# One encoder layer on one core: the first value tiles are computed token tile by token tile, ahead of the queries and keys

## The reference

```python
u = rmsnorm(h, g_pre_mix)
proj = u @ w_in                       # 512 x 3840
qa, ka, va, qb, kb, vb, qc, kc, vc = split(proj)
ya = diff_attention(qa, ka, va, ...)  # branch A: 4 heads, two softmaxes each
yb = sliding_window_sink_attention(qb, kb, vb, ...)   # branch B: 8 heads
yc = chunk_band_attention(qc, kc, vc, ...)            # branch C: 8 heads
mixed = gates[0] * (ya @ w_proj_a) + gates[1] * (yb @ w_proj_b) + gates[2] * (yc @ w_proj_c)
h = h + rmsnorm(mixed @ w_out, g_post_mix)
h = h + rmsnorm(conv_ffn(rmsnorm(h, g_pre_ffn), ...), g_post_ffn)
```

## Time and profile before

| | |
|---|---|
| time, median of 3 runs | 844.48 us (843.78 to 846.26) |
| the profiled execution | 843.84 us, its span 842.0 us |
| TensorE busy | 833.5 us (99%) |
| VectorE busy | 653.8 us (78%) |
| ScalarE busy | 481.5 us (57%) |
| GpSimd busy | 400.1 us (48%) |
| DMA | 111.35 MB, mean 132 GB/s |

### The profile page before, as it was taken

The page is one execution under the profiler, slowest core; times in us unless marked ns, Lnnn a source line. Parts: engine busy times, 40 slices in busy tenths (PEclk is TensorE's granted clock), DMA queues, the critical chain, the costliest instruction groups (busy, mean ns, idle before and its releaser), DMA issues.

```text
span 842.0 us, 13461 instructions
## 1 busy us (share of the span) xinstructions
PE 833.5 (99%) x4721; PEld 729.3 (87%) x4721; DVE 653.8 (78%) x1257; ACT 481.5 (57%) x906; POOL 400.1 (48%) x511
## 2 busy tenths in 40 slices
PE   8999999999999999999999999999999999999997
PEld 7888888888888888999998889899999999988885
DVE  6678877788866767966544389988888888999996
ACT  6566666777666664544444447456565656545662
POOL 5554443334444446987667435756565656010002
PEclk9999999999999999999999999999999999999999
DMA  8542223233233212333335641555553433396584
GB/s 229 158 121 55 64 86 99 75 98 82 83 82 81 62 41 88 113 110 110 107 101 206 198 147 51 172 175 179 162 178 112 131 110 129 132 329 219 172 285 157
DMA packets 139079, 111.35 MB, mean 132 GB/s; under 512 B 7591, under 2 KB 122223, under 8 KB 137732
## 3 DMA queue, kind: packets, MB, share of 16 engines
q1 hardware_dynamic: 137386, 102.05, 39.8%
q0 software_dynamic: 720, 5.24, 1.7%
q10 hardware_dynamic: 906, 3.20, 1.0%
HBM read 97.05 MB, written 13.42 MB: 131 GB/s over the span
## 4 chain that ended last, share of the span: by engine, by line
PE 94%; DVE 2%; POOL 1%; DMA 1%; ACT 1%; issue 1%; DVEq 0%; SPq 0%; ACTq 0%
PE banks L2280 23%; PE banks L2282 23%; PE banks L2281 23%; PE banks L2557 3%; PE banks L2556 3%; PE banks L2555 3%; PE banks L2456 2%; PE banks L2365 2%; PE banks L2364 2%; PE banks L2726 1%; PE banks L2725 1%; PE banks L2724 1%; PE banks L2428 1%; PE banks L2435 1%; PE banks L2419 1%; DVE scratch L1976 1%
## 5 line engine op out<-in xcount | busy, mean ns | idle before, releaser
L856 POOL TENSOR_TENSOR ring_lo<-ring_raw,ring_hi 128x256 fp32r<-128x256 f32 x376 | 307.2, 850 | 262.8 <-ACT ring_hi L1014 262.4
L2280 PE MATMUL banks<-u_hi,ring_hi 128*128 128x512 f32 (+1 forms) x612 | 231.3, 378 | 0.5 <-POOL ring_lo L880 0.5
L2282 PE MATMUL banks<-u_hi,ring_lo 128*128 128x512 f32 (+1 forms) x612 | 226.4, 370 | 0.0
L2281 PE MATMUL banks<-u_lo,ring_hi 128*128 128x512 f32 (+1 forms) x612 | 226.1, 370 | 0.0
L2282 PEld LDWEIGHTS banks<-u_hi,ring_lo 128*128 128x128 f32 x612 | 115.2, 188 | 20.2
L2280 PEld LDWEIGHTS banks<-u_hi,ring_hi 128*128 128x128 f32 x612 | 115.4, 189 | 18.6 <-DVE u_lo L1587 0.8
L2281 PEld LDWEIGHTS banks<-u_lo,ring_hi 128*128 128x128 f32 x612 | 115.6, 189 | 18.0
L1014 ACT CAST ring_hi<-ring_raw 128x1024 fp32r<-128x1024 f32 x95 | 98.9, 1044 | 37.4 <-PE banks L2282 24.1
L2101 DVE SCALAR_TENSOR_TENSOR wide<-banks,cols,wide 128x511 f32<-128x511 f32 x88 | 64.6, 745 | 3.5 <-ACT wide L1374 1.6
L2280 PE MATMUL banks<-pages,ring_hi 128*128 128x512 f32 (+1 forms) x180 | 61.2, 340 | 0.0
L2281 PE MATMUL banks<-pages,ring_hi 128*128 128x512 f32 (+1 forms) x180 | 61.2, 340 | 0.0
(11 more groups left out here) (325 smaller groups left out, 1991.9 us busy)
## 6 DMA issues: line engine op xcount, KB each, us to landing
ring_raw<-in_w_ffn_up_dram SPq DMA_DIRECT2D x88, 256.0 KB, 3.6
ring_raw<-in_w_in_dram SPq DMA_DIRECT2D x60, 256.0 KB, 3.4
ring_raw<-in_w_ffn_down_dram SPq DMA_DIRECT2D x55, 256.0 KB, 3.6
ring_raw<-in_w_gate_dram SPq DMA_DIRECT2D x48, 256.0 KB, 3.2
split_tokens<-pages SPq DMA_DIRECT2D x5, 1024.0 KB, 7.0
pages<-split_tokens POOLq DMA_DIRECT2D x5, 1024.0 KB, 6.5
ring_raw<-in_w_out_dram SPq DMA_DIRECT2D x16, 256.0 KB, 3.1
second_tokens<-wide SPq DMA_DIRECT2D x10, 384.0 KB, 3.9
```

Source lines behind the costliest of these rows:

```text
L856: last = pool.tensor_tensor(wlo[:, r, c], raw[:, r, c], whi[:, r, c].bitcast(F32), ALU.subtract)
L2280: pe.matmul(out, lhs_hi, rhs_hi, start=start, stop=False)
L2281: pe.matmul(out, lhs_hi, rhs_lo, start=False, stop=False)
L2282: return pe.matmul(out, lhs_lo, rhs_hi, start=False, stop=stop)
```

## The change

- Tiles 0 and 1 of the order are `va` and `vb`: the values of units 0 and 1 together, 256 feature columns wide, with rows 0 to 511 of the weights in `va` and rows 512 to 1023 in `vb`.
- Their products (`value_products`) take the tokens as the stationary operand, a token tile of 128 at a time, and 256 weight columns as the moving one. The result stands by tokens, so `v_feat`, `turn_v` and `v_parts` fall away for units 0 and 1; `first_values` evacuates from the bank to the value pages.
- Token tile 0 is turned alone, in two halves, then tiles 1, 2 and 3, each between products of the tiles before.
- SyncE loads x tile 0, then `va`, x tile 1, `vb`, x tiles 2 and 3, then the next two weight tiles. ScalarE rounds tile 0 before it squares token tile 1. The square of token tile 2 is VectorE's.
- Query and key of unit 0 follow at full width (512 tokens), and then `qk(0)`. Four tiles are now computed ahead of the slots, and two more (`SPLIT_AHEAD`) are split ahead of them. The slots get other cuts.
- Idle transposes: 11, 4 and 1 where there were 14, 2 (four times) and 6. Some small loads share a semaphore.

```diff
-SLOT_CUTS = {"A": (0, 5, 11, 17, 24), "C": (0, 5, 10, 16, 24), "B": (0, 6, 11, 17, 24)}
-WARM_UP = (14, 2, 6)
+GEMM_ORDER = ("va0 vb0 q0 k0 q1 k1 v2 q2 k2 v3 q3 k3 v4 q4 k4 v5 q5 k5 v6 q6 k6 v7 q7 k7 v8 k8 q8 "
+              "gate0 q9 gate1 gate2 q10 gate3 gate4 q11 gate5 gate6 gate7")
+SLOT_CUTS = ((0, 5, 11, 17, 23),) + 3 * ((0, 5, 11, 17, 24),) + 4 * ((0, 5, 10, 17, 24),) + (
+    (0, 6, 11, 17, 23), (0, 5, 11, 16, 22), (0, 5, 11, 16, 22), (0, 3, 7, 10, 14))
+SPLIT_AHEAD = RING + 2
+WARM_UP = (11, 4, 1)
...
+        def first_values(g, part, h):
+            page = pages[:, v_page(h, part), :]
+            return tiled(page)[:, g::2, :], psum[:, proj_bank(g), :].rearrange("p (t h n) -> p t h n", t=2, h=2)[:, :, h, :]
...
             load_x(0)
-            load_x(1)
-            load_x(2)
...
+            def by_k_wide(t, r, src):
+                dst = raw[:, r, :].rearrange("p (k n) -> p k n", n=2 * P)
+                load(t, r, (dst[:, 0:2, :], dst[:, 2:4, :]), (src[:, 0:2, :], src[:, 2:4, :]))
...
                 if t == 1:
+                    load_x(1)
+                if t == 2:
+                    load_x(2)
                     load_x(3)
...
             rstd(0, 0)
-            rstd(0, 1)
-            rstd(0, 2)
-            pool.wait_ge(first_half_hi, 1)
+            pool.wait_ge(w_hi_done, 1)
             w_lo_quarter(0, 0)
             w_lo_quarter(0, 1)
-            pool.wait_ge(w_hi_done, 1)
+            rstd(0, 1)
             w_lo_quarter(0, 2)
-            w_lo_quarter(0, 3)
+            w_lo_quarter(0, 3).then_inc(w_lo_done, 1)
+            pool.wait_ge(w_hi_done, 2)
+            w_lo_quarter(1, 0)
+            rstd(0, 2)
...
             square(0, 0, x_tok[:, 0, :])
+            w_hi_at(0)
             act.wait_ge(x_loaded[1], 16)
             square(0, 1, x_tok[:, 1, :])
...
+            act.wait_ge(first_turned, 1)
+            act.copy(u_hi[:, 0:4, 0:P], turned_tokens(0, 0)[:, 0:4, :]).then_inc(u_first_hi, 1)
+            act.wait_ge(xs_turned, 1)
+            act.copy(u_hi[:, 4:8, 0:P], turned_tokens(0, 0)[:, 4:8, :]).then_inc(u_hi_done, 1)
+            w_hi_at(1)
+            u_high(1, 0)
             act.wait_ge(x_loaded[3], 16)
+            act.wait_ge(squares, 3)
             square(0, 3, x_tok[:, 3, :])
-            w_hi_at(1)
+            w_hi_at(2)
             u_high(2, 0)
             u_high(3, 0)
-            w_hi_at(2)
             w_hi_at(3)
...
+            proj_out(0)
             act.wait_ge(lam_dots, 2)
             act.activation(lam_exp[:], lam_dot[:], ACT.Exp).then_inc(lam_exps, 1)
-            proj_out(0)
             proj_out(1)
+            w_hi_at(RING)
             act.wait_ge(dist_done, 2)
...
+            for t in range(RING + 1, SPLIT_AHEAD):
+                w_hi_at(t)
             proj_out(2)
+            proj_out(3)
...
+            xs(0, 1, x_tok[:, 1, :], spread_gain())
+            dve.wait_ge(x_loaded[2], 16)
+            dve.tensor_tensor_reduce(tmp, x_tok[:, 2, :], x_tok[:, 2, :], 1.0, 0.0, ALU.mult, ALU.add,
+                                     norm_ss[:, 0, 2:3]).then_inc(squares, 1)
+            u_low(1, 0)
             for t in (2, 3):
                 xs(0, t, x_tok[:, t, :], spread_gain())
...
+                if kind in ("va", "vb"):
+                    dve.wait_ge(proj_act, g + 1)
+                    for h in range(2):
+                        lo, half = first_values(g, 1, h)
+                        last = dve.tensor_tensor(lo, half, first_values(g, 0, h)[0].bitcast(F32), sub)
+                    last.then_inc(v_lo, 1)
+                    return
...
             tables()
-            for g in range(3):
+            for g in range(RING):
                 proj_low(g)
...
                     pe.wait_ge(proj_act, g - 1)
+                    if g <= RING:
+                        pe.wait_ge(v_lo, 2)
...
+            def value_products(t, u_part, w_part, ks):
+                dst = psum[:, proj_bank(t % 2), 2 * P * (t // 2):2 * P * (t // 2 + 1)]
+                for k in ks:
+                    mm = pe.matmul(dst, u_part[:, k, t * P:(t + 1) * P],
+                                   w_part[:, k // 4, 2 * P * (k % 4):2 * P * (k % 4 + 1)],
+                                   start=u_part is u_hi and w_part is whi and k == 0,
+                                   stop=w_part is wlo and k == KT - 1)
+                return mm
...
+            pe.wait_ge(u_first_hi, 1)
+            pe.wait_ge(w_hi_done, 1)
+            value_products(0, u_hi, whi, first)
+            pe.wait_ge(u_first_lo, 1)
+            value_products(0, u_lo, whi, first)
+            pe.wait_ge(u_hi_done, 1)
+            pe.wait_ge(w_hi_done, 2)
+            value_products(0, u_hi, whi, second)
+            pe.wait_ge(u_lo_done, 1)
+            value_products(0, u_lo, whi, second)
+            pe.wait_ge(w_lo_done, 1)
+            value_products(0, u_hi, wlo, first)
+            turn_tokens(1, 0, x_tok[:, 1, :])
+            pe.wait_ge(u_hi_done, 2)
+            value_products(1, u_hi, whi, both)
+            pe.wait_ge(u_lo_done, 2)
+            value_products(1, u_lo, whi, both)
+            value_products(1, u_hi, wlo, first)
+            turn_tokens(2, 0, x_tok[:, 2, :])
+            pe.wait_ge(w_lo_done, 2)
+            value_products(0, u_hi, wlo, second)
+            value_products(1, u_hi, wlo, second)
+            pe.wait_ge(u_hi_done, 3)
+            value_products(2, u_hi, whi, both)
+            turn_tokens(3, 0, x_tok[:, 3, :])
+            pe.wait_ge(u_lo_done, 3)
+            value_products(2, u_lo, whi, both)
+            value_products(2, u_hi, wlo, both).then_inc(tile_used, 1)
+            turn_tables()
+            pe.wait_ge(u_hi_done, 4)
+            value_products(3, u_hi, whi, both)
+            pe.wait_ge(u_lo_done, 4)
+            value_products(3, u_lo, whi, both)
+            value_products(3, u_hi, wlo, both).then_inc(tile_used, 1)
             gemm_steps(STEPS[-1][2 * KT:])
...
-                if qt == 0 and u <= 8:
+                if qt == 0 and 2 <= u <= 8:
                     turn_v(u)
```

More of the change, by code:

```diff
@@ L464, in build_encoder @@
         x_loaded = [sem(f"x_loaded{t}") for t in range(TT)]
-        small_loaded = [sem(f"small_loaded{i}") for i in range(9)]
+        small_loaded = [sem(f"small_loaded{i}") for i in range(7)]
         raw_loaded = [sem(f"raw_loaded{r}") for r in range(RING)]
@@ L697, in _ @@
             for u in range(4, UNITS - 1):
-                bias_before[min(t for t in range(2 * RING, T_ATT) if split_slot(t - RING) >= TT * (u - 1))] = u
+                later = [t for t in range(2 * RING, T_ATT) if split_slot(t - RING) >= TT * (u - 1)]
+                bias_before[min(later, default=T_ATT)] = u
             for t, (kind, n) in enumerate(TILES):
@@ L902, in _ @@
             pool.wait_ge(mask_done, 1)
+            for t in range(RING, SPLIT_AHEAD):
+                w_lo(t, t % RING)
             for s in range(SLOTS):
@@ L1180, in _ @@
                     w_hi_at(t)
-                for g in range(3, T_ATT):
+                for g in range(RING, T_ATT):
                     if FINISH[g] == s and (TILES[g][0] == "q" and u >= 8):
@@ L2315, in _ @@
             for part in range(2):
-                for t in range(2):
-                    keep_clock_up(WARM_UP[1])
-                    pe.wait_ge(xs_done if part else xs_first, t + 1)
-                    for k in range(4):
-                        last = pe.transpose(first_turned(part)[:, k, t * P:(t + 1) * P],
-                                            x_tok[:, t, (4 * part + k) * P:(4 * part + k + 1) * P], ident[:])
-                last.then_inc(xs_turned, 1)
-            keep_clock_up(WARM_UP[2])
+                keep_clock_up(WARM_UP[1 + part])
+                pe.wait_ge(xs_done if part else xs_first, 1)
+                for k in range(4 * part, 4 * part + 4):
+                    last = pe.transpose(turned_tokens(0, 0)[:, k, :], x_tok[:, 0, k * P:(k + 1) * P], ident[:])
+                last.then_inc(xs_turned if part else first_turned, 1)
             def bank_free(g):
@@ new lines, in _ @@
+            first, second, both = range(4), range(4, KT), range(KT)
+            pe.wait_ge(u_first_hi, 1)
[9 more added lines that the diff above has]
+            pe.wait_ge(w_lo_done, 1)
```

146 lines of the change are left out of this document (55 added, 91 removed).

## The result

| | before | after |
|---|---|---|
| median | 844.13 us (4 runs) | 849.32 us (846.75 to 851.34, 4 runs) |
| ratio | | 1.0056, 95% interval 1.0037 to 1.0074 |
| the profiled execution | 843.84 us, span 842.0 | 846.75 us, span 844.9 |
| TensorE busy | 833.5 us | 832.1 us |

The change made the kernel slower, by 0.56%. Forecast were 848.0 us, 847.3 for the profiled execution.

What follows compares the result with a forecast made beforehand. TensorE was taken as the bound (94% of the span). Start +0.3, wait 1 +1.2, wait 2 +2.9 and transposes -0.9 gave +3.45 us; against the median 844.48, 848.0 us was expected, range 845.2 to 850.7.

Steps and rivals of the forecast that it cites:

- The matmul work: TensorE's gemm stream: columns move between tiles but their number stays, 304 k-steps before and after; difference nothing.
- The start, +0.3: Up to the end of the 96 small matmuls: 27.35 against 27.06 us, the 2.3 us gained in front spent in gaps.
- the ring: Start, per token tile: TensorE transposes, ScalarE copies, VectorE subtracts and scales in turn; 4.4 us a round against 3.8 of TensorE work.
- Wait 1: Before k0: TensorE waits 1.2 us for bank 7, until VectorE, after `tables()`, has the values' low parts done at 33.95.
- Wait 2: Before `qk(0)`: TensorE stands still 2.9 us for k0's evacuation by ScalarE and VectorE, which nothing covers; `qk(0)` at 42.35.
- Transposes, -0.9: Units 0 and 1: `turn_v`, eight transposes at 0.11 us, falls away; saves 0.9 us.
- the equal point: The start of `qk(0)` at which nothing is gained or lost: 32.53 plus v1 (5.47) and two `turn_v` (0.9), 38.9 us.
- Slots at nothing: Slots lose eight k-steps and two `turn_v` over the same softmax chain; taken as zero, bound +2 us.
- the thin place: Slot 46: probabilities ready 0.9 us before TensorE wants them; the change takes one k-step (0.68) from that slot.
- The clock as a rival: Standstill before `qk(0)` or gaps from 7 to 15 us bring TensorE's clock down: 2.5 us more, 850.5; chance 0.06.

Runs made afterwards that it cites:

- the turns: Against the kernel after: token tiles 1 and 2 are transposed ahead of the four products that stood before them; 849.09 us, ratio 1.0066.
- the square: Square of token tile 1 moved from ScalarE to VectorE, against the kernel with three k-steps and token transposes moved ahead and k evacuated by halves; 843.8 us, ratio 1.0002.
- 2.1 us of cover: Against the kernel after: three k-steps of q1 put ahead of `qk(0)`, taken out of slots 0 to 3; 845.48 us, ratio 1.0021.
- the 4.2 us of standstill: Against the kernel after: two more VectorE passes over k0's bank before its subtractions; 850.86 us. With 34 idle transposes added in that wait: 850.17 us.
- the wait filled: Against the kernel after: 24 idle transposes put ahead of `qk(0)`, the wait itself as long; 849.11 us, ratio 1.0063.

## Why the prediction was right, and where it was not

The forecast, 848.0 us and slower, holds: 849.32 and 848.6 in two sets, both in the range. Step by step:

- **The matmul work is the same.** Right: after `qk(0)` nothing new shows but slot 46.
- **The start, +0.3.** Right: +0.39 (27.45 against 27.06). The first product came at 9.42 (9.65 forecast), the gap at tile 1 was 1.10 (1.3), and the 2.6 us of head start went into gaps. Both kernels that worked on the ring bear it out: a gap taken away at one engine comes back in part at the next, 0.65 us of gain by the turns and 0.4 of 1.7 by the square. Of the two pages cited, the Trainium skill (DMA: Bandwidth & Descriptors, Why small descriptors are slow) would have had the first weight tile 0.15 us earlier than the 6.1 of my sum; its rounding began at 6.48, and in other profiles of the same loads between 6.30 and 7.66, so the runs can't show so small an effect.
- **Wait 1, k0 for its bank, +1.2.** The term that was wrong: mis-sized, it measured nothing. I took 7.6 us for `tables()` from the earlier trace rows and moved it by 5 us unchanged. But that price held 29 copies slowed by GpSimd, which was splitting two weight tiles at that time; after the change that work lies elsewhere, `tables()` takes 5.0 us, and the values are done at 31.0, 1.9 us before TensorE wants bank 7 for k0 (32.92). The mechanism of the wait is real: with GpSimd kept busy it appears, 1.6 us.
- **Wait 2, `qk(0)` for k0, +2.9.** Right: 2.78 us of wait, 41.30 at `qk(0)`, and 2.1 us of cover take 2.1 us off the wait.
- **Transposes, -0.9.** Not tested by the 2.4 us at `qk(0)`, since the equal point of 38.9 already holds the term. From start to start a `turn_v` of the kernel before takes 0.36 us (36.39 to 36.75 and 58.29 to 58.65), so the two were worth 0.7 and not 0.9, and the equal point was 38.7.
- **Slots at nothing.** Nearly: slot 46 waits 0.2 us, the thin place of the earlier trace rows. From `qk(0)` to slot 47 the loss grows by 0.7 us, and by the end 0.2 comes back. Of the half microsecond left, 0.2 is the transposes' size; the rest is not traced to a row.
- **The clock as a rival with 6 in 100.** Too low as a chance that it falls at all, near in its price. It did not fall in the profiled execution, so the sum for that one came out near (846.75 against 847.3). That it can fall there is shown: by filling the 4.2 us of standstill the clock stayed up, and the fall had cost 1.57 us, where I had put 1.6 for one spell; after 2.8 us it fell in one profile of four. The Trainium skill (TensorE: Matmul & The Clock Gate, HAM oscillation) says that idle gaps let the clock fall and the next burst pays; these two records agree, the three others with 2.8 us do not.
- **How much of it is in the medians is not shown.** Of nine executions of the kernel after, those with a mean clock of 0.998 or 0.999 took 846.75, 847.65, 847.76 and 851.34 us, those with 0.996 or 0.997 took 848.6 to 849.8. One spell of 3.4 us at half clock is 1.7 us lost, two thousandths of the mean, so a fall in some executions fits. Against it as the main cause: with the wait filled the median stayed at 849.1, with two of six at 0.997; and one execution with the wait at 0.7 us had 0.996, so such a mean is no proof of a fall before `qk(0)`. Two other things lengthen single executions: the late landing of x tile 1, up to 1.3 us, and the passing wait of the feed-forward stage, 1.5 to 2.4 us. The kernel before has longer executions as well, 16 of 71 over 845 us, all with mean clocks of 0.998 or more, so a median of four or five moves with their share.

So the profiled execution came out near with one term too large (1.2 us in wait 1) and half a microsecond of loss behind `qk(0)` that was not in the sum; and the median came out near partly by luck, since what lifts the executions that were not profiled, 849.2 to 851.3, was not in the sum and is only in part explained. The 851.34 at a mean clock of 0.998 is not explained at all.

## What to carry to other kernels

When a reorder puts the producer of an operand last, right ahead of its first use, the evacuation that other work used to cover is paid in full: count it before the saved instructions. A price read from a trace holds for the neighbours it had there; when a step is moved, ask what GpSimd does beside VectorE in the old place and the new one. A standstill of TensorE near 3 us can cost its own length and then a spell at half clock (1.6 us here), not in every execution, so look at the clocks of all runs and not at the one profile.

## What the runs showed that I had not expected

- VectorE's small float32 copies from page to page: 0.15 us for 12x4 and 12x7 with GpSimd idle, 0.39 and 0.54 on average with GpSimd subtracting, single ones up to 0.70; 12x1 stayed at 0.131 and GpSimd's subtractions at 0.73. The Trainium skill (SBUF — State Buffer, SBUF: two separate sides) says that a VectorE operation that uses both port pairs and a GpSimd operation exclude each other for a whole instruction. The 0.70, about one subtraction, agrees; the untouched 12x1 copies show that the form decides.
- The clock after a standstill of TensorE: 2.8 us left it at 1.00 in three profiles and brought it to 0.5 in one; 4.2 us brought it to 0.5 for 3.4 us; 1.6 and 2.8 us, with 6 us of work between them, for about 7. What tells the four with 2.8 us apart is open.
- A wait of 1.2 us in the feed-forward stage, near 795 us, for ScalarE's copies into a bank. It is in three of the thirteen profiles of the kernel after and its variants, which differ nowhere behind slot 47, and there puts TensorE's end 1.5 to 2.4 us later. Why it comes and goes was not tried.
- The third load of the queue, x tile 1: the square that waits for it started between 7.75 and 9.02 us in profiles of one load order.
